# A three-layer transformer kernel on one core: gate rows read back from DRAM, and fewer closing steps on TensorE

## The chip, the cores and the metric

One of the cores of a Trainium2 chip runs the whole program. The metric is the device time of one execution in microseconds (us); lower is better. The core has TensorE (PE; its weight loads are shown apart as PEld), VectorE (DVE), ScalarE (ACT), GpSimd (POOL) and SyncE (SP), and 16 DMA engines that all queues share.

## The reference, cut to what matters

Two blocks run one after the other on a sequence of 256 tokens of width 1024. The first has two attentions and 16 experts. The second, in which the change lies, is this:

```python
for i in range(2):
    shift, scale, gate = adaln_params(c, ada_w[i, 0], ada_b[i, 0])
    hn = modulate(h, norm_g[i, 0], shift, scale)
    m = s5_mixer(hn, ...) if i == 0 else fox_mixer(hn, ...)
    h = h + gate * m
    shift, scale, gate = adaln_params(c, ada_w[i, 1], ada_b[i, 1])
    hn = modulate(h, norm_g[i, 1], shift, scale)
    h = h + gate * conv_ffn(hn, ...)
# end of s5_mixer:   y = gelu(y);  y = y * sigmoid(y @ w_glu);  return y @ w_out
# conv_ffn:          a, b = split(h @ w_up);  return (silu(conv3(a)) * b) @ w_down
```

The `gate` is one row of 1024 numbers for each of the four layers (S5, feed-forward 0, fox attention, feed-forward 1), the same for all tokens.

## The kernel before, in words

The stages run in this order: input projections and the two attentions of the first block; routing and 16 experts, whose weights stream from DRAM; S5; feed-forward 0; fox attention; feed-forward 1; the last norm. Each engine runs a list of instructions written out by hand, with waits on semaphores between the engines. TensorE's multiplications all go through the helper `mm` (line 705), its transposes of normed rows through `turn` (line 712).

**Weights.** They go through a ring of six slots of 2 MB. SP issues the loads in one fixed order (`weight_plan`), and each waits until the step that used its slot last is through (`released`). A weight is then split in two float32r parts, high on ACT (`apart_high`, line 508), low on DVE (`apart_low`, line 516), and TensorE makes three products (high by high, low by high, high by low) for each product of the reference. The two blocks of the S5 output weight are called ("s5", 4) and ("s5", 5). The second goes to the slots that ("s5", 2) had, the first block of `w_glu`, so it is loaded once `glu_mm` has reached 2.

**End of S5.** `y` comes in eight pieces, `ct` 0 to 7. Its first four and its last four are split separately: `y_high` on ACT (lines 1919, 1923), `y_low` on DVE (line 2807). The sums of `y @ w_glu` are made by `glu(i, half)`: `i` is the block of `w_glu`, `half` says which half of `y` goes in, and only the call with half 1 raises `glu_mm`, twice. ACT then makes the sigmoid of each bank (line 1931), DVE the product and its parts (lines 2844 to 2846), and TensorE multiplies by the output weight in four groups of 24 products, (t, n) = (0, 0), (0, 1), (1, 0), (1, 1). During S5 six blocks of `ada_w`, the weight behind shift, scale and gate, are loaded and multiplied (`ada_product`), one for each `ct`.

**Gate rows.** The results stand in `mod`, spread over partitions: element 128 c + p of a gate is on partition p. To multiply rows of tokens by it, it is needed as a row on every partition. `gate_rows` makes that on TensorE, with a product by the identity for each of 8 pieces, into two banks of PSUM, and ACT copies them to `GBs`, `GB` or `GBx` (lines 1927, 1968, 2031; `GB` and `GBx` are the tensor `adaS`). The DVE function `add_gated` (lines 2773 and 2774) multiplies a sum by the row and adds it to the residual `X`.

**Feed-forward.** 22 tiles of 128 columns, two to a step of the loop. For each tile TensorE has 48 products of `up` and 12 of `down`; ACT copies (line 1974) and makes the silu (1976), DVE the convolution, the product and its parts (2890 to 2898), and both split the next weights (1942, 1949; 2856, 2862). The four sums of `down` stay in banks 4 to 7 through all tiles. They are opened by a product of zeros in bf16 and closed by another one (`closed`), which raises `ffn_mm`; the closing products stand between the groups of three of the last tile.

Of the kernel before, what the change touches and what calls it, by code (L numbers as in the profile page):

```python
# [20 lines left out]
F32 = mybir.dt.float32  # L21
# [223 lines left out]
def build(nc, x, cons, cols, rows, relb, wrt, wff, bf16z, w_in, w_qb, w_kvb, w_o, w_gate, w_up, w_down, ada_w,  # L245
# [3 lines left out]
    sums_dram = nc.dram_tensor("forget_sums", [FH, T], F32).ap()  # L249

    with ExitStack() as ctx:
# [250 lines left out]
        def apart_high(act, n, halves=(0, 1)):  # L502

            name = APART[n]
            act.wait_ge(filled_sem[slot_of[name]], filled_at(*name))
            for half in halves:
                a = slice(half * SLOT // 2, (half + 1) * SLOT // 2)
                act.activation(ringr[:, high_slot[name], a], ring[:, slot_of[name], a], ACT.Copy  # L508
                               ).then_inc(S("w_high"), 1)
# [72 lines left out]
        def _(sp):  # L582
# [36 lines left out]
            for name, i in order:  # L619
                if name == "w_in":  # L620
                    a, n = Z_COLS[i]
                    s = begin(name, i)
                    if i == 0:
                        h = NC // 2 * n
                        sp.dma_start(ring[:, s, 0:h], w_in[:, 0:h]).then_inc(S("w_in_half"), 16)
# [49 lines left out]
                elif name == "s5":  # L675
                    load(begin(name, i), SLOT, block((s5_in, s5_glu, s5_out)[i // 2], i % 2))
# [20 lines left out]
        def _(pe):  # L697
# [93 lines left out]
            def gate_rows(layer, banks):  # L791

                for c in range(NC):
                    last = mm(ps[:, banks[c // 4], (c % 4) * P:(c % 4) * P + P],
                              mod[:, layer, 16 + c:17 + c].to_broadcast([P, P]), ident, True, True)
                last.then_inc(S("gate_mm"), 1)

# [17 lines left out]
            pe.wait_ge(S("w_in_half"), 16)  # L815
# [534 lines left out]
            glu(1, 0)  # L1350
            pe.wait_ge(S("mod_ready"), 1)
            pe.wait_ge(S("ada_kept"), 5)
            gate_rows(0, (6, 7))
            pe.wait_ge(S("y_low"), 2)
            glu(0, 1)
            glu(1, 1)


            pe.wait_ge(S("gate_copied"), 1)
# [20 lines left out]
            def ffn(k, turned):  # L1380
# [35 lines left out]
                def down(i, b, closing=False):  # L1416
                    pe.wait_ge(S("down_low"), i * 2 + (NF * k + b + 1))
                    pe.wait_ge(S("g_ready"), i * 2 + (NF * k + b + 1))
                    for i4 in range(4):
                        n, t = (i4 % 2, i4 // 2) if closing else (i4 // 2, i4 % 2)  # L1420
                        for g, w in ((gh, dh), (gl, dh), (gh, dl)):
                            last = mm(ps[:, 4 + 2 * n + t, :], g[:, b, t * P:t * P + P],
                                      w[:, b, BANK * n:BANK * n + BANK], False, False)
                        if closing and i4 < 3:
                            closed(4 + 2 * n + t)
                    last.then_inc(S("down_mm"), 1)
                    if closing:
                        closed(7)

                def closed(b):  # L1430

                    mm(ps[:, b, :], zb[0:1, 0:P], zb[0:1, :], False, True).then_inc(S("ffn_mm"), 1)
# [3 lines left out]
                gate_rows(2 * k + 1, (2, 3))  # L1436
# [64 lines left out]
            gate_rows(2, (2, 3))  # L1501
# [4 lines left out]
            pe.wait_ge(S("gate_copied"), 3)  # L1506
# [25 lines left out]
        def _(act):  # L1532
# [53 lines left out]
            def both_halves(k, r, layer, high):  # L1586
# [6 lines left out]
                for t in range(NT):  # L1593
                    features_high(k, t, high)

# [308 lines left out]
            for ct in range(NC):  # L1904
# [22 lines left out]
            act.activation(GBs.rearrange("p (b n) -> p b n", b=2), ps[:, 6:8, :], ACT.Copy  # L1927
                           ).then_inc(S("gate_copied"), 1)
# [6 lines left out]
            def ffn(k, turned, layer, roots, beside):  # L1935
# [9 lines left out]
                def down_high(i, b, first=False):  # L1945
                    ffn_filled(act, "down", k, b, i)
                    if not first:
                        act.wait_ge(S("down_mm"), i * 2 + (NF * k + b - 1))
# [18 lines left out]
                act.wait_ge(S("gate_mm"), layer + 1)  # L1967
                act.activation(GB.rearrange("p (b n) -> p b n", b=2), ps[:, 2:4, :], ACT.Copy
                               ).then_inc(S("gate_copied"), 1)
# [51 lines left out]
            def values_copied(j):  # L2021
# [8 lines left out]
            act.wait_ge(S("gate_mm"), 3)  # L2030
            act.activation(GBx.rearrange("p (b n) -> p b n", b=2), ps[:, 2:4, :], ACT.Copy
                           ).then_inc(S("gate_copied"), 1)
            values_copied(1)

# [188 lines left out]
        def _(v):  # L2223
# [626 lines left out]
            v.wait_ge(S("gate_copied"), 1)  # L2850

            def ffn(k, turned, layer, roots, added, beside):
# [61 lines left out]
                v.wait_ge(S("gate_copied"), layer + 1)  # L2914
# [61 lines left out]
            fox_low(7)  # L2976

# [105 lines left out]
```

## Time and profile before

| | us |
|---|---|
| median of three runs | 1316.57 (1311.68 to 1319.81) |
| the profiled execution | 1316.12 |
| its span | 1314.3 |
| mean granted clock of TensorE in it | 0.954 of full speed |

The profiled execution is longer than its span by 1.8 us, which lie around it. Busy time is what an engine did, not what bounds the kernel; the waits and the chain that ended last say that.

### The profile page before, as it was taken

To read this page: it belongs to the slowest core of one execution; us is meant where nothing else is said; L and a number is where in the kernel's file an instruction comes from. 1 tells how busy PE (TensorE), PEld (TensorE's weight loads), DVE (VectorE), ACT (ScalarE), POOL (GpSimd) and SP (SyncE) were. 2 spreads that over 40 slices of the span, in tenths; PEclk is the share of its full clock that TensorE was granted. 3 is DMA by queue.
4 is the path that set the end of the run, shared out by engine and by line. 5 is a ranking of instruction groups with operands and counts; after the bars stand their busy time and mean duration, and the time that the engine had idled before them with its cause. 6 is when DMAs were issued, how large, how long until landed. Compare 5 with 4: busy or idle time off the path is not lost.

```text
span 1314.3 us, 22196 instructions
## 1 busy us (share of the span) xinstructions
PE 1191.1 (91%) x8874; PEld 851.7 (65%) x8874; DVE 669.4 (51%) x1207; ACT 462.2 (35%) x746; POOL 168.1 (13%) x270
## 2 busy tenths in 40 slices
PE   8999899887789877787999999999999989999996
PEld 5646554432335323332877889999969767999995
DVE  3677452231211221121486757676675766667675
ACT  5463421010100001002654454444455545443343
POOL 0000115572343032101020000000000000000000
PEclk9999899898987899798999999999999999999998
DMA  9865599999999999999786465555456241554441
GB/s 372 356 222 244 230 404 418 430 428 428 428 428 428 428 429 428 429 428 428 291 349 231 161 272 203 181 191 191 176 193 240 82 160 49 187 192 184 178 178 40
DMA packets 38389, 371.81 MB, mean 283 GB/s; under 512 B 4133, under 2 KB 7742, under 8 KB 14398
## 3 DMA queue, kind: packets, MB, share of 16 engines
q1 hardware_dynamic: 34462, 365.47, 68.8%
q10 hardware_dynamic: 3872, 5.57, 1.2%
q8 instruction: 39, 0.64, 0.2%
q14 instruction: 16, 0.13, 0.0%
HBM read 369.94 MB, written 1.08 MB: 282 GB/s over the span
## 4 chain that ended last, share of the span: by engine, by line
PE 66%; DMA 23%; DVE 5%; ACT 3%; issue 2%; POOL 1%; DVEq 0%; SPq 0%; ACTq 0%
PE ps L705 64%; DMA ring<-in_w_up 20%; DMA ring<-in_ada_w 2%; PE ps L936 1%; DMA ring<-in_fox_out 1%; DMA ring<-in_s_out 1%; ACT XH L1617 1%; DVE X L2774 1%; DVE ring_parts L516 1%; ACT XH L1575 0%; PE ps L712 0%; DVE W L2955 0%; DMA X<-in_x 0%; PE ps L948 0%; DVE XH L2773 0%
## 5 line engine op out<-in xcount | busy, mean ns | idle before, releaser
L705 PE MATMUL ps<-W_parts 128*128 128x256 f32 (+2 forms) x2672 | 383.9, 305 | 3.9 <-DVE W_parts L2898 2.0
L705 PEld LDWEIGHTS ps<-W_parts 128*128 128x128 f32 x2672 | 356.8, 191 | 28.0 <-issue 4.1
L705 PE MATMUL ps<-ring,W 128*32 128x512 f32 (+2 forms) x1512 | 239.3, 679 | 55.2 <-DMA ring<-in_w_up 29.1
L705 PEld LDWEIGHTS ps<-ring,W 128*32 128x32 f32 (+1 forms) x1512 | 62.1, 124 | 190.8 <-issue 114.6
L705 PE MATMUL ps<-W 128*32 128x64 f32 (+7 forms) x1696 | 135.6, 290 | 23.9 <-DVE W L2755 12.8
L705 PEld LDWEIGHTS ps<-W 128*32 128x32 f32 (+5 forms) x1696 | 85.6, 152 | 78.3 <-issue 70.8
L2743 DVE COPY W<-ps 128x1024 f32<-128x1024 f32 x16 | 19.6, 1224 | 191.4 <-PE ps L705 191.4
L2856 DVE TENSOR_TENSOR W_parts<-ring,W_parts 128x2048 fp32r<-128x2048 f32 x44 | 100.8, 2292 | 26.2 <-ACT W_parts L1942 26.0
L705 PEld LDWEIGHTS ps<-kc,W 128*128 128x128 f32 x648 | 85.7, 212 | 28.2 <-DVE W L2743 17.4
L705 PE MATMUL ps<-kc,W 128*128 128x32 f32 (+2 forms) x648 | 88.1, 293 | 10.2 <-DVE W L2743 9.4
L705 PE MATMUL ps<-XH_parts,ring_parts 128*128 128x256 f32 x512 | 94.0, 286 | 2.1 <-ACT XH_parts L1578 1.9
L705 PEld LDWEIGHTS ps<-XH_parts,ring_parts 128*128 128x128 f32 x512 | 80.7, 193 | 6.0 <-ACT XH_parts L1578 3.9
L1942 ACT ACTIVATE W_parts<-ring 128x2048 fp32r<-128x2048 f32 x44 | 83.6, 1900 | 0.1
L516 DVE TENSOR_TENSOR ring_parts<-ring,ring_parts 128x2048 fp32r<-128x2048 f32 x27 | 60.8, 2283 | 25.4 <-ACT ring_parts L508 25.4
L705 PE MATMUL ps<-W_parts,ring_parts 128*128 128x256 f32 x256 | 73.1, 285 | 0.0
L705 PE MATMUL ps<-ring_parts,W_parts 128*128 128x512 f32 (+1 forms) x256 | 72.0, 397 | 1.0 <-DVE ring_parts L516 1.0
L508 ACT ACTIVATE ring_parts<-ring 128x2048 fp32r<-128x2048 f32 x28 | 52.4, 1907 | 30.3 <-DMA ring<-in_fox_in 12.5
L1828 ACT ACTIVATE W<-ps 128x1024 f32<-128x1024 f32 x16 | 16.4, 1023 | 126.6 <-PE ps L705 126.6
L2761 DVE TENSOR_TENSOR X<-X,ps 128x512 f32<-128x512 f32 x64 | 44.0, 687 | 28.9 <-PE ps L705 28.7
L1974 ACT ACTIVATE XH<-ps 128x256 f32<-128x256 f32 x44 | 16.8, 383 | 115.5 <-PE ps L705 115.5
L1847 ACT ACTIVATE W<-ps 128x512 f32<-128x512 f32 x16 | 9.6, 597 | 134.0 <-PE ps L705 134.0
L705 PEld LDWEIGHTS ps<-ring_parts,W_parts 128*128 128x128 f32 x256 | 47.8, 189 | 11.7 <-DVE ring_parts L516 1.4
(395 smaller groups left out, 1353.5 us busy)
## 6 DMA issues: line engine op xcount, KB each, us to landing
ring<-in_w_up SPq DMA_DIRECT2D x32, 2048.0 KB, 25.7
ring<-in_w_down SPq DMA_DIRECT2D x32, 2048.0 KB, 23.7
ring<-in_w_gate SPq DMA_DIRECT2D x29, 2048.0 KB, 24.0
ring<-in_ada_w SPq DMA_DIRECT2D x24, 2048.0 KB, 10.1
ring<-in_up SPq DMA_DIRECT2D x44, 1024.0 KB, 5.8
ring<-in_dn SPq DMA_DIRECT2D x44, 512.0 KB, 3.3
ring<-in_fox_in SPq DMA_DIRECT2D x6, 2048.0 KB, 7.9
ring<-in_w_o SPq DMA_DIRECT2D x2, 2048.0 KB, 15.7
```

Source lines behind the costliest of these rows:

```text
L508: act.activation(ringr[:, high_slot[name], a], ring[:, slot_of[name], a], ACT.Copy).then_inc(S("w_high"), 1)
L516: eng.tensor_tensor(ringr[:, slot_of[name], a], ring[:, slot_of[name], a], ringr[:, high_slot[name], a].bitcast(F32), ALU.subtract).then_i ...
L705: return pe.matmul(o, l, r, start=a, stop=z_, skip_group_check=True, **kw)
L936: last = pe.transpose(ps[:, 4 + g % 2, o:o + P], Pex[:, 2 * (g % 4) + h, kb * P:kb * P + P], ident)
L1617: act.activation(Pex[:, h, 0:n], src, ACT.Exp, bias=ngm[:, u, h:h + 1], scale=scale, accum_out=den[:, u, h:h + 1]).then_inc(S("exp_done"), 1)
L1828: act.activation(Gs.rearrange("p (b n) -> p b n", b=2), ps[:, 0:2, :], ACT.Copy).then_inc(S("g_copied"), 1)
L1942: act.activation(uh[:, b], ffn_raw("up", k, b).rearrange("p (a n) -> p a n", a=2), ACT.Copy).then_inc(S("up_high"), 1)
L1974: act.activation(apd[:, b, 2:2 + T], ps[:, b, 0:T], ACT.Copy).then_inc(S("a_copied"), 1)
L2743: v.tensor_copy(Us.rearrange("p (b n) -> p b n", b=2), ps[:, 2:4, :]).then_inc(S("u_copied"), 1)
L2761: tt(xs_part, xs_part, ps[:, k, :], ALU.add).then_inc(S("x_added"), 1)
L2774: tt(X[:, t, a], X[:, t, a], normed_rows[k][:, t, a], ALU.add).then_inc(S("x_gated"), 1)
L2856: tt(ul[:, b, :, :], ffn_raw("up", k, b).rearrange("p (a n) -> p a n", a=2), uh[:, b, :, :].bitcast(F32), ALU.subtract).then_inc(S("up_low ...
```

## The change

- `gate_rows`, its 8 products a layer and ACT's copies are gone. In their place ACT issues, for each layer, a DMA that writes the gate from `mod` to a new DRAM tensor (`gate_written`; the elements lie 4 bytes by 4 bytes: partition p holds elements p, 128 + p, ...) and later one that reads it back as a row onto 128 partitions (`gate_spread`). Layer 0 is written at `ct` 1 of S5 and read after the last `y_high`; layers 1 and 2 are written after the first two tiles of feed-forward 0, layer 3 after those of feed-forward 1; layers 1 and 3 are read before the last two tiles of their feed-forward, layer 2 after `values_copied(1)` of the fox stage.
- TensorE no longer waits for `gate_copied`; DVE does, at one more place (before the fox sums are added).
- The last of the three products of each closing group carries the closing mark and raises `ffn_mm`; `closed` is gone.
- ("s5", 5) is loaded in two halves with a semaphore each, and ACT splits its first half when that one is there.
- The gate sums of S5 go in the order glu(0, 0), glu(0, 1), glu(1, 0), glu(1, 1). Before: glu(0, 0), glu(1, 0), gate_rows, glu(0, 1), glu(1, 1).

```diff
@@ S5 on TensorE
-            glu(1, 0)
-            pe.wait_ge(S("mod_ready"), 1)
-            pe.wait_ge(S("ada_kept"), 5)
-            gate_rows(0, (6, 7))
             pe.wait_ge(S("y_low"), 2)
             glu(0, 1)
+            glu(1, 0)
             glu(1, 1)
-            pe.wait_ge(S("gate_copied"), 1)
+            pe.wait_ge(S("ada_kept"), 5)
@@ down, last tile
-                        for g, w in ((gh, dh), (gl, dh), (gh, dl)):
+                        for j, (g, w) in enumerate(((gh, dh), (gl, dh), (gh, dl))):
                             last = mm(ps[:, 4 + 2 * n + t, :], g[:, b, t * P:t * P + P],
-                                      w[:, b, BANK * n:BANK * n + BANK], False, False)
-                        if closing and i4 < 3:
-                            closed(4 + 2 * n + t)
-                    last.then_inc(S("down_mm"), 1)
-                    if closing:
-                        closed(7)
+                                      w[:, b, BANK * n:BANK * n + BANK], False, closing and j == 2)
+                        if closing:
+                            last.then_inc(S("ffn_mm"), 1)
+                    if not closing:
+                        last.then_inc(S("down_mm"), 1)
@@ feed-forward and fox on TensorE
                 up(0, 0, True)
-                gate_rows(2 * k + 1, (2, 3))
...
             values(0, 0, 0, 0, NC)
-            gate_rows(2, (2, 3))
             values(1, 0, 1, 0, NC)
...
-            pe.wait_ge(S("gate_copied"), 3)
@@ ACT
+            def gate_written(layer):
+                act.dma_start(bass.AP(gate_dram.tensor, layer * D, [[1, P], [P, NC]]), mod[:, layer, 16:24],
+                              allow_slow_non_contiguous=True).then_inc(S("gate_written"), 16)
+            def gate_spread(dst, layer, written):
+                act.wait_ge(S("gate_written"), 16 * written)
+                act.dma_start(dst, gate_dram[layer].partition_broadcast(P)).then_inc(S("gate_copied"), 16)
...
+                if ct == 1:
+                    gate_written(0)
...
+            gate_spread(GBs, 0, 1)
             apart_high(act, 4)
-            act.wait_ge(S("gate_mm"), 1)
-            act.activation(GBs.rearrange("p (b n) -> p b n", b=2), ps[:, 6:8, :], ACT.Copy
-                           ).then_inc(S("gate_copied"), 1)
...
                 tiles(0, True, True)
+                act.wait_ge(S("mod_ready"), 2 + k)
+                for row in (1, 2) if k == 0 else (3,):
+                    gate_written(row)
                 with act.Fori(1, NF // 2 - 1) as i:
                     tiles(i, True)
+                gate_spread(GB, layer, 3 + k)
                 tiles(NF // 2 - 1, False)
```

## Rows read from the trace of the kernel before

**Rows 1.** The page: the chain that ended last, by engine, share of the span.

```profile
PE 66%; DMA 23%; DVE 5%; ACT 3%; issue 2%; POOL 1%; DVEq 0%; SPq 0%; ACTq 0%
```

**Rows 2.** Windows, the feed-forwards: busy (x), granted clock, DMA share, GB/s.

```profile
772.00:960.00 188.00, 187.00 (x1327) 176.09 (x1327) 131.22 (x178) 82.17 (x93) 0.00 (x0) 1.00 0.52 195
1113.00:1301.00 188.00, 186.76 (x1326) 176.13 (x1327) 129.20 (x178) 80.01 (x91) 0.00 (x0) 1.00 0.44 162
```

**Rows 3.** Timeline of TensorE, gate rows: start, us, line, tiles; S5, feed-forward 0, fox.

```profile
726.80 1.95 PE L705 MATMUL ps<-kc,mod 128*128 128x128 f32 x16
...
777.81 1.95 PE L705 MATMUL ps<-kc,mod 128*128 128x128 f32 x16
...
1030.29 1.95 PE L705 MATMUL ps<-kc,mod 128*128 128x128 f32 x16
```

**Rows 4.** Timeline of DVE: the last `y_low`.

```profile
722.29 1.23 DVE L2807 TENSOR_TENSOR W_parts<-XH,XH_parts 128x1024 fp32r<-128x1024 f32 x1 [7.30 <-ACT XH_parts L1923]
```

**Rows 5.** Timeline of TensorE: start of glu(1, 0), then the S5 output groups.

```profile
720.96 0.36 PE L705 MATMUL ps<-XH_parts,ring_parts 128*128 128x256 f32 x1
...
739.89 5.75 PE L705 MATMUL ps<-ring_parts,W_parts 128*128 128x512 f32 x24
746.66 11.47 PE L705 MATMUL ps<-ring_parts,W_parts 128*128 128x512 f32 x48 [1.01 <-DVE ring_parts L516]
```

**Rows 6.** The chain that ended last, in order of time, around ("s5", 5).

```profile
734.47 7.86 DMA ring<-in_s_out
742.36 1.93 ACT ring_parts L508
```

**Rows 7.** Windows of 1 us around an idle time of TensorE; columns as in rows 2.

```profile
628.00:629.00 1.00, 0.00 (x0) 0.00 (x0) 0.92 (x3) 0.97 (x3) 0.00 (x0) 1.00 1.06 442
629.00:630.00 1.00, 0.20 (x2) 0.23 (x3) 1.00 (x2) 1.00 (x3) 0.00 (x0) 1.00 1.04 442
...
631.00:632.00 1.00, 1.00 (x7) 1.00 (x6) 0.08 (x1) 1.00 (x2) 0.00 (x0) 0.50 1.08 459
```

**Rows 8.** Timeline, the end of feed-forward 0: TensorE and DVE.

```profile
959.25 0.94 PE L705 MATMUL ps<-W_parts 128*128 128x512 f32 x3 [1.00 <-DVE W_parts L2898]
960.12 0.38 PE L705 MATMUL ps<-zb 1*128 1x512 bf16 x1
960.44 0.97 PE L705 MATMUL ps<-W_parts 128*128 128x512 f32 x3
960.61 0.69 DVE L2773 TENSOR_TENSOR W<-ps,adaS 128x512 f32<-128x512 f32 x1 [1.51 <-PE ps L705]
...
964.08 3.64 PE L705 MATMUL ps<-ring,silz 128*32 128x512 f32 x32
...
965.32 0.69 DVE L2774 TENSOR_TENSOR X<-X,W 128x512 f32<-128x512 f32 x1
```

**Rows 9.** Timeline of TensorE, the first fox scores.

```profile
1038.72 1.16 PE L705 MATMUL ps<-W 64*128 64x128 f32 x16 [0.90 <-DVE W L2955]
```

**Rows 10.** DMA queue q10 (ACT's): packets, MB, share; 998 to 1003 and 1003 to 1018.

```profile
q10 hardware_dynamic: 32, 0.02, 1.2%
...
q10 hardware_dynamic: 2064, 2.10, 42.4%
```

**Rows 11.** S5, an `ada_w` block: its issue, its time to landing, its product.

```profile
672.37 0.33 SPq L596 DMA_DIRECT2D ring<-in_ada_w  x1
...
ring<-in_ada_w SPq DMA_DIRECT2D x1, 2048.0 KB, 9.4
...
684.27 1.93 PE L705 MATMUL ps<-ring,silz 128*32 128x512 f32 x16
```

**Rows 12.** Feed-forward 0, an `up` tile: issue, time to landing, use on ACT.

```profile
789.74 0.34 SPq L616 DMA_DIRECT2D ring<-in_up  x1
...
ring<-in_up SPq DMA_DIRECT2D x1, 1024.0 KB, 7.5
...
797.93 1.90 ACT L1942 ACTIVATE W_parts<-ring 128x2048 fp32r<-128x2048 f32 x1
```

More of the change, by code:

```diff
@@ L249, in build @@
     sums_dram = nc.dram_tensor("forget_sums", [FH, T], F32).ap()
+    gate_dram = nc.dram_tensor("gate_rows", [LAYERS, D], F32).ap()
     with ExitStack() as ctx:
@@ L504, in apart_high @@
             name = APART[n]
-            act.wait_ge(filled_sem[slot_of[name]], filled_at(*name))
             for half in halves:
+                if name == ("s5", 5) and half == 0:
+                    act.wait_ge(S("half_filled"), 32)
+                else:
+                    act.wait_ge(filled_sem[slot_of[name]], filled_at(*name))
                 a = slice(half * SLOT // 2, (half + 1) * SLOT // 2)
@@ L624, in _ @@
                         h = NC // 2 * n
-                        sp.dma_start(ring[:, s, 0:h], w_in[:, 0:h]).then_inc(S("w_in_half"), 16)
+                        sp.dma_start(ring[:, s, 0:h], w_in[:, 0:h]).then_inc(S("half_filled"), 16)
                         sp.dma_start(ring[:, s, h:2 * h], w_in[:, h:2 * h]).then_inc(filled_sem[s], 16)
@@ L675, in _ @@
                 elif name == "s5":
-                    load(begin(name, i), SLOT, block((s5_in, s5_glu, s5_out)[i // 2], i % 2))
+                    src = block((s5_in, s5_glu, s5_out)[i // 2], i % 2)
+                    if i == 5:
+                        s = begin(name, i)
+                        sp.dma_start(ring[:, s, 0:SLOT // 2], src[:, 0:SLOT // 2]).then_inc(S("half_filled"), 16)
+                        sp.dma_start(ring[:, s, SLOT // 2:], src[:, SLOT // 2:]).then_inc(filled_sem[s], 16)
+                    else:
+                        load(begin(name, i), SLOT, src)
                 elif name == "up0":
@@ L789, in features @@
                             last.then_inc(S(sem), 1)
[L791 to L796, printed above, removed]
             pe.wait_ge(S("zeroed"), 1)
@@ L814, in _ @@
             wz = ring[:, slot_of["w_in", 0], :].rearrange("p (c n) -> p c n", c=NC)
-            pe.wait_ge(S("w_in_half"), 16)
+            pe.wait_ge(S("half_filled"), 16)
             pe.wait_ge(S("ht_act"), 1)
@@ L1947, in down_high @@
                     if not first:
-                        act.wait_ge(S("down_mm"), i * 2 + (NF * k + b - 1))
+                        act.wait_ge(S("down_mm"), i * 2 + ((NF - 1) * k + b - 1))
                     act.activation(dh[:, b, :], ffn_raw("down", k, b), ACT.Copy
@@ L1966, in ffn @@
                 down_high(0, 0, True)
-                act.wait_ge(S("gate_mm"), layer + 1)
-                act.activation(GB.rearrange("p (b n) -> p b n", b=2), ps[:, 2:4, :], ACT.Copy
-                               ).then_inc(S("gate_copied"), 1)
                 def tiles(i, ups, first=False):
@@ L2029, in _ @@
             apart_high(act, 12)
-            act.wait_ge(S("gate_mm"), 3)
-            act.activation(GBx.rearrange("p (b n) -> p b n", b=2), ps[:, 2:4, :], ACT.Copy
-                           ).then_inc(S("gate_copied"), 1)
             values_copied(1)
+            gate_spread(GBx, 2, 3)
             def fox_high(u):
@@ L2849, in _ @@
                 apart_low(v, 5, half)
-            v.wait_ge(S("gate_copied"), 1)
+            v.wait_ge(S("gate_copied"), 16)
             def ffn(k, turned, layer, roots, added, beside):
@@ L2913, in ffn @@
                 tiles(NF // 2 - 1, False)
-                v.wait_ge(S("gate_copied"), layer + 1)
+                v.wait_ge(S("gate_copied"), 16 * (layer + 1))
                 for j in range(4):
@@ L2976, in _ @@
             fox_low(7)
+            v.wait_ge(S("gate_copied"), 48)
             def fox_added(t, n):
```

2 lines of the change are left out of this document (removed).

## The prediction

> **What bounds the kernel now.** I read the page first: the chain of work that ended last goes through TensorE for 66% of the span, through DMA for 23%, through DVE for 5% [rows 1]. The DMA part is the experts' stage, which the change doesn't touch. Then the windows by stage: in both feed-forwards TensorE is busy 187 of 188 us at full clock, while the DMA engines are busy about half of the time [rows 2]. So there a product taken off TensorE is time taken off the kernel, and one more DMA is cheap. At the seams between the stages (end of S5, end of each feed-forward, start of the fox scores) it is the other way round: TensorE waits for DVE or ACT there, and a product taken off it only makes it wait longer. Each part of the change has to be read at its own place.
>
> **Gate rows off TensorE.** Each `gate_rows` is 8 products, seen as 16 passes, and takes 1.95 us [rows 3]. There are four.
> - Feed-forward 0 and 1: the products lie between the first and the second tile of `up`, in a stretch in which TensorE never rests [rows 2]. Gain 1.95 us each, 3.9 us together. What would be late next is the second tile's weights or the first tile's convolution; both have the 5.6 us of the next `up` tile before them and ACT loses its 1.03 us copy there, so I count nothing against the gain.
> - Fox: the products end at 1032.2, but the scores start at 1038.72 and wait 0.90 us for the last mask sum on DVE [rows 3, 9], whose chain has nothing to do with the gate rows. TensorE will wait 0.90 + 1.95 = 2.85 us instead. Gain 0.
> - S5: the products go, but so does the order around them (next part).
> - Added: four writes and four reads, issued by ACT. An issue of a DMA there costs its queue about 0.4 us; ACT has idle times of 2 us and more at each of these places, the copies of about 1.03 us that it loses are longer, and the reads land long before DVE needs them: 512 KB at S5 some 25 us ahead, in the feed-forwards two tiles, some 15 us. Cost 0, unless the writes hold up other loads (first rival). SP's list is not moved; nothing is queued on it behind the new DMAs except through the shared engines.
>
> **The order of the gate sums.** Before, glu(1, 0) starts at 720.96 [rows 5] and hides the wait for the second half of `y`: the last `y_low` runs on DVE from 722.29 for 1.23 us, so it is there at 723.5 [rows 4]. After, glu(0, 1) is next in line and TensorE must wait from 720.96 to about 723.6: 2.6 us. All the 144 products behind it are the same. Before, the sums and the gate rows end at 739.89 [rows 5]; that is 720.96 + 1.95 + 16.98 for three half sums. After: 723.6 + 17.0 = 740.6. So the new order loses 0.7 us at this point: the wait takes more than the place of the gate rows.
> In return `glu_mm` 2 comes at 723.6 + 5.6 = 729.2 and not at 734.4, and with it the load of ("s5", 5), which was issued at 734.47 and took 7.86 us [rows 6]. That load was late: ACT waited for it until 742.36, and TensorE stood 1.01 us at the second output group for the low part [rows 5, 6]. After, it has landed by about 737 in either form, so halving it adds nothing that the earlier start doesn't give. ACT splits it after the last sigmoid, from 741.3; the first half passes ACT (1.9 us) and DVE (2.3 us) by 745.5; the first output group ends at 740.6 + 5.75 = 746.3. The wait of 1.01 us goes. Net at the end of S5: +0.7 - 1.0 = -0.3 us.
>
> **The clock behind that wait.** The trace shows what a short rest of TensorE can do: after the windows 628 to 630, in which it was busy 0.20 of 2 us, it was at full clock first and then at 0.50 (1.2 in place of 2.4 GHz) in the window 631 to 632 [rows 7], in all for some 3.3 us. That costs about 1.65 us where TensorE sets the time. The page "TensorE: Matmul & The Clock Gate" of the Trainium skill (Part 1) says that the throttled clock is the default and that activity lifts it; the trace agrees in this row. The change adds three such rests: 2.6 us before glu(0, 1), 2.85 us before the fox scores, and one at the end of feed-forward 0 (below). The closest row is a rest of 1.8 us, and there the clock fell; so I take a fall in S5, +1.7 us. In the fox stage it already falls once after the scores begin; earlier or later makes no sure difference, 0 with 1.7 us either way.
>
> **The closing products.** A closing group is three products at 0.24 us each; with the product of zeros the groups start 1.19 us apart (959.25, 960.44) [rows 8]. Without it they start 0.72 us apart. But DVE takes 1.33 us for each of the four sums, so only the first one counts: DVE starts at 960.61, just after the zeros end at 960.50; in the change the third product ends at 960.19, so it starts at 960.30. Gain 0.31 us in each feed-forward, 0.6 us together. At the end of feed-forward 0 TensorE comes to the `ada_w` products (3.64 us, at 964.08 before [rows 8]) 1.9 us earlier and then has nothing to do for 2.1 us before the transposes: the third rest. I count no fall there; it is close.
>
> **Sum.** 3.9 (feed-forwards) + 0.3 (S5) + 0.6 (closings) = 4.8 us gained, 1.7 lost to the clock: 3.1 us net. Against the profiled execution: 1316.12 - 3.1 = 1313.0. This execution is 0.45 us under the median of the three runs (1316.57), which is nothing beside their spread of 8 us, so I leave the number at 1313.0.
>
> **Rival 1, slower: the writes of the gate rows choke the loads.** A gate is written in 1024 pieces of 4 bytes, 64 for each DMA engine. No row shows such a write. The nearest: ACT's queue moved 32 packets, half of them of 1 KB, in 1.2% of 16 x 5 us, 30 ns each, and 2064 packets of 1 KB in 42.4% of 16 x 15 us, 49 ns each [rows 10]. With p for one piece, a write takes 64 p of every engine. In S5 it falls into a row of loads with a slack of 684.27 - (672.37 + 9.4) = 2.5 us [rows 11]; in the feed-forward an `up` tile lands at 797.2 and is used at 797.93 [rows 12], and TensorE is a further 3.0 us behind ACT, together 3.7 us, for two writes in feed-forward 0 and one in feed-forward 1. Cost: (64 p - 2.5) + (128 p - 3.7) + (64 p - 3.7), each part at least 0. At 30 ns it is 0.1 us; at 49 ns 0.6 + 2.6 = 3.2 us; I take nothing, since a piece of 4 bytes carries less than the packets of both rows, and keep 3.2 us for the range. At p = 65 ns it would be 1.7 + 4.6 + 0.5 = 6.8 us, more than all the gain; this is where it decides. At 100 ns: 3.9 + 9.1 + 2.7 = 15.7 us, a time of 1328.7. At 120 ns 1334.
> The page "DMA: Bandwidth & Descriptors" of the Trainium skill speaks for this rival: by its rules for kernel authors a non-contiguous last dimension becomes one descriptor per element, and by its specifications a transfer under 512 B is done as a read, a change and a write. It gives no time for such an element; if that doubled the price of 49 ns, the time would be that of 100 ns above. No run of before shows such a write.
>
> **Rival 2: no fall of the clock.** The rest in S5 may lie so that the clock stays up: the trace has a rest of TensorE before the fox scores of 0.90 us without one, and the fall in rows 7 followed a rest that was cut in two. Then 1316.1 - 4.8 = 1311.3.
>
> **Rival 3: the gain is eaten.** The clock falls in S5 and again behind the 2.1 us rest after feed-forward 0 (3.3 us together), and a load is late by 1 to 2 us. Then 1316.1 - 4.8 + 3.3 + 1.5 = 1316.1, no change.
>
> **Rival 4: more than counted.** The clock stays up in S5 and the fall that the fox stage now has goes too, so that the second half of its chain, which hangs on a product made at half clock, moves up by 1.7 us, and the feed-forwards lose a wait or two of ACT: about 1309.
>
> **How the numbers follow.** Forecast with one fall 0.40; no fall 0.25; eaten 0.17; choked loads 0.09 (0.04 of it by less than 13 us above before); more than counted 0.09. The likeliest gives 1313. The range from 1308.5 to 1318 takes in all but the choked loads and the outer part of the runs' own spread. A measurement of this kernel can tell about 1% (13 us) from no change: faster by more than that would need 1303, which no case gives, 0.03; slower by more needs p of about 0.12 us, 0.05; within it 0.92.
>
> **What would show each step.** In the changed profile: no `ps<-kc,mod` rows; TensorE busy all through both feed-forwards, each 1.95 us shorter from its first `up` product to its last; a wait of TensorE for DVE line 2807 of about 2.6 us before glu(0, 1), and the window after it at 0.5 or at 1.0; the second output load issued near 729 and no wait for its low part; DVE's four sums starting 0.1 us after the third product; the fox scores starting after the same mask sum, with 2.9 us of rest before them; 1024 packets more for each gate, and their busy time, which gives p. The prediction is wrong if TensorE waits for an `ada_w` block in S5 or for a split weight in feed-forward 0, or if the reads of the gate rows come after DVE wants them.

## The result: slower by half a per cent, against a forecast of a small gain

The changed kernel takes 1323.98 us in the median of 17 runs (1316.32 to 1329.39), the kernel before 1316.9 us (17 runs, 1311.68 to 1323.1): a ratio of 1.0054, 95% interval 1.0036 to 1.0071. The forecast was 1313.0 us with a range up to 1318. So it is within 1% of the time before, but on the wrong side of it: 11.0 us above the forecast and 6.0 us above the end of the range.

The profiled execution of the changed kernel spans 1319.8 us against 1314.3 us. To see where the 5.5 us come from, I take the same TensorE products in both timelines as landmarks and write down the time from one to the next. The landmarks: the `ada_turn` products (`ps<-kc,adaS`) in S5, at 661.36, 702.01 and 720.04 us before, and the one after feed-forward 0, at 985.59; the first product of the S5 output [rows 5]; the first `up` product and the end of the last `down` product of each feed-forward; the first fox scores [rows 9].

| stretch, from landmark to landmark | before, us | after, us | difference |
|---|---|---|---|
| S5: `ada_turn` 1 to `ada_turn` 2 | 40.65 | 47.77 | +7.12 |
| `ada_turn` 2 to `ada_turn` 3 | 18.03 | 17.82 | -0.21 |
| `ada_turn` 3 to S5 output (the gate sums) | 19.85 | 22.15 | +2.30 |
| S5 output to first `up` | 32.10 | 30.82 | -1.28 |
| feed-forward 0, first `up` to last `down` | 191.84 | 189.03 | -2.81 |
| from there to its `ada_turn` | 21.76 | 23.05 | +1.29 |
| to the first fox scores | 53.13 | 53.03 | -0.10 |
| fox scores to first `up` | 74.52 | 72.83 | -1.69 |
| feed-forward 1 | 191.83 | 191.12 | -0.71 |
| from there to the end | 9.23 | 10.50 | +1.27 |

With 0.3 us that the execution is late at the first landmark already, these add up to 5.5 us. In the stretch from the fox scores to the first `up` TensorE waits for nothing that the change moved; it takes 72.8 to 76.2 us from one kernel's profile to another, with the granted clock in it at 0.98 to 0.91, so its 1.69 us are no gain of the change. The largest loss, more than the whole difference, is in one stretch that the forecast had at zero. Feed-forward 1 is the second place: it gained 0.71 us where feed-forward 0 gained 2.81.

**S5, the write of a gate row.** The page first, the chain that ended last, by engine:

```profile
PE 62%; DMA 24%; DVE 7%; ACT 3%; issue 2%; POOL 1%; SPq 0%; DVEq 0%; ACTq 0%
```

TensorE's share is lower than in [rows 1] (62% and 66%), DMA's and DVE's are a little higher. That fits work that waits for data; the rows below show where. The timeline of the changed kernel, rows that answer to [rows 11]: SP's issue of the `ada_w` block, ACT's issue of the write, TensorE, and the block's product:

```profile
672.70 0.33 SPq L600 DMA_DIRECT2D ring<-in_ada_w  x1
...
673.92 0.40 ACTq L1590 DMA_DIRECT2D gate_rows<-mod  x1
...
687.57 4.13 PE L715 MATMUL ps<-W 32*128 32x64 f32 x32 [0.24 <-issue]
691.62 3.19 PE L715 MATMUL ps<-ring,silz 128*32 128x512 f32 x16
```

The DMA view of the issues in 672 to 675: KB each, us from issue to landing:

```profile
ring<-in_ada_w SPq DMA_DIRECT2D x1, 2048.0 KB, 14.9
```

The block was issued 0.33 us later than in [rows 11] and its product ran 7.35 us later; it landed after 14.9 us and not after 9.4. The windows between (TensorE, its weight loads, DVE, ACT, POOL, clock, DMA share, GB/s):

```profile
674.00:682.00 8.00, 6.09 (x152) 4.32 (x149) 7.79 (x15) 2.94 (x5) 1.40 (x2) 1.00 0.87 332
682.00:684.00 2.00, 1.02 (x33) 0.85 (x25) 0.69 (x2) 0.00 (x0) 0.00 (x0) 1.00 3.20 131
684.00:686.00 2.00, 0.66 (x12) 0.56 (x13) 0.00 (x0) 1.37 (x3) 1.33 (x2) 1.00 0.00 0
686.00:688.00 2.00, 0.88 (x11) 0.73 (x14) 0.00 (x0) 1.65 (x3) 0.07 (x1) 0.85 0.53 41
688.00:692.00 4.00, 4.00 (x36) 3.41 (x36) 2.74 (x6) 0.00 (x0) 0.00 (x0) 0.50 0.59 221
```

and the queues in the first two of them:

```profile
q10 hardware_dynamic: 1014, 0.00, 7.1%
...
q1 hardware_dynamic: 16, 0.26, 319.0%
```

The prediction had no row for such a write; here it is. 1014 packets of 4 bytes took 7.1% of 16 x 8 us, 9 ns each, less than either price in [rows 10]. And still the loads stop. The 16 load packets that begin in 682 to 684, 16 KB each, took 319% of 16 x 2 us, 6.4 us each; in 684 to 686 no further packet begins (share 0.00, 0 GB/s). TensorE, ACT and POOL run dry, and after that idle time the clock is at 0.50. The price of the write is not its pieces' own time; it is the time by which the loads under way land later. I call this the hold.

The same hold meets the `up` tile in feed-forward 1, whose write was issued at 1134.01. ACT and TensorE:

```profile
1147.74 1.92 ACT L1943 ACTIVATE W_parts<-ring 128x2048 fp32r<-128x2048 f32 x1 [6.19 <-DMA ring<-in_up]
...
1152.04 8.31 PE L715 MATMUL ps<-W_parts 128*128 128x256 f32 x58 [2.36 <-DVE W_parts L2856]
```

The tile landed after 14.4 us. TensorE waits 2.36 us; in feed-forward 0 only 0.29 us, although there are two writes; there the two `up` tiles beside them landed after 12.3 and 12.8 us. An `up` tile took 7.5 us in [rows 12], so both feed-forwards have the hold, and most of it fits in the slack between a tile's landing and its use.

**The gate sums**, answering to [rows 4, 5, 7]: the last `y_low`, the wait before glu(0, 1), and the windows behind it.

```profile
729.52 1.23 DVE L2807 TENSOR_TENSOR W_parts<-XH,XH_parts 128x1024 fp32r<-128x1024 f32 x1 [7.08 <-ACT XH_parts L1927]
```

```profile
730.80 0.50 PE L715 MATMUL ps<-XH_parts,ring_parts 128*128 128x256 f32 x2 [2.47 <-DVE W_parts L2807]
```

```profile
732.00:734.00 2.00, 2.00 (x11) 2.00 (x11) 1.93 (x5) 1.98 (x2) 0.00 (x0) 0.50 0.00 0
734.00:736.00 2.00, 2.00 (x15) 2.00 (x14) 2.00 (x2) 0.90 (x2) 0.00 (x0) 0.70 0.03 8
```

The forecast wait was 2.6 us, the profile has 2.47, and the clock falls to 0.50 behind it, as forecast.

**The ends of the feed-forwards**, answering to [rows 8, 9]: the last group in one run of 12 products, DVE's first sum, the `ada_w` products; then the fox scores.

```profile
966.29 2.98 PE L715 MATMUL ps<-W_parts 128*128 128x512 f32 x12 [1.00 <-DVE W_parts L2898]
967.33 0.69 DVE L2773 TENSOR_TENSOR W<-ps,adaS 128x512 f32<-128x512 f32 x1 [1.19 <-PE ps L715]
...
969.20 3.64 PE L715 MATMUL ps<-ring,silz 128*32 128x512 f32 x32
...
974.98 1.97 PE L722 MATMUL ps<-kc,W 128*128 128x128 f32 x16 [2.13 <-ACT W L1559]
...
1045.35 1.70 PE L715 MATMUL ps<-W 64*128 64x128 f32 x16 [2.57 <-DVE W L2955]
```

DVE starts 1.04 us after the group where it was 1.36 us [rows 8]; the rest before the transposes is 2.13 us (forecast 2.1); the scores wait 2.57 us (forecast 2.85).

### The profile page after: what moved, and what is told of

It is laid out like the page before. It is cut to its first block, busy times and chain, and to the rows that moved or that the text cites. A ratio compares the mean times of both kernels' runs of the same rounds, so it can differ in the third digit from the quotient of the medians.

```text
span 1319.8 us, 22056 instructions
## 1 busy us (share of the span) xinstructions
PE 1186.0 (90%) x8802; PEld 846.4 (64%) x8802; DVE 670.1 (51%) x1207; ACT 458.6 (35%) x742; POOL 168.7 (13%) x270
## 4 chain that ended last, share of the span: by engine, by line
PE 62%; DMA 24%; DVE 7%; ACT 3%; issue 2%; POOL 1%; SPq 0%; DVEq 0%; ACTq 0%
PE ps L715 60%; DMA ring<-in_w_up 13%; DMA ring<-in_w_gate 6%; DMA ring<-in_up 2%; DMA ring<-in_s_in 2%; PE ps L939 1%; DMA ring<-in_fox_out 1%; ACT XH L1619 1%; DVE X L2774 1%; ACT XH L1567 0%; PE ps L722 0%; DVE W L2955 0%; DMA X<-in_x 0%; PE ps L951 0%; DVE W_parts L2856 0%
## 5 line engine op out<-in xcount | busy, mean ns | idle before, releaser
L715 PE MATMUL ps<-ring,W 128*32 128x512 f32 (+2 forms) x1512 | 242.4, 685 | 53.9 <-DMA ring<-in_w_up 29.3
L715 PE MATMUL ps<-W 128*32 128x64 f32 (+7 forms) x1696 | 138.4, 294 | 28.4 <-DVE W L2755 12.8
L1830 ACT ACTIVATE W<-ps 128x1024 f32<-128x1024 f32 x16 | 16.4, 1024 | 126.3 <-PE ps L715 126.3
```

The lines of the kernel that those rows point to most:

```text
L715: return pe.matmul(o, l, r, start=a, stop=z_, skip_group_check=True, **kw)
L1830: act.activation(Gs.rearrange("p (b n) -> p b n", b=2), ps[:, 0:2, :], ACT.Copy).then_inc(S("g_copied"), 1)
```

## The experiments

Theory A: the writes in 4-byte pieces hold the loads that share the engines with them. The rival to it is B: the loss belongs to the new order, the halves or late instructions. And for how the hold comes about there are three forms of A. A1: pieces that lie next to each other in DRAM; A2: their number; A3: any small write. Each run was timed beside the kernel before on the same chip (medians of before 1316.8 to 1317.3 us).

**1. Rows in 512-byte pieces.**

```diff
+                mm(ps[0:m, bank, 0:P], modf[:, 24 * l0 + 16:24 * l1], ident, True, True)
...
-                act.dma_start(bass.AP(gate_dram.tensor, layer * D, [[1, P], [P, NC]]), mod[:, layer, 16:24],
-                              allow_slow_non_contiguous=True).then_inc(S("gate_written"), 16)
+                own(act.activation(gT[0:m, :], ps[0:m, bank, 0:P], ACT.Copy))
+                act.dma_start(gate_dram[l].rearrange("(c n) -> c n", c=NC), gT[r:r + NC, :]
```

> The changed kernel, but the rows go out in other pieces: one product with the identity turns the 8 gate columns of a layer into 8 rows of 128 numbers (one for layer 0, one for layers 1 and 2, one for layer 3), ACT copies them out of PSUM, and each layer is written as 8 pieces of 512 bytes in place of 1024 pieces of 4 bytes. Everything else, the reads of the rows included, stays. Theory A (the 4-byte writes hold the loads behind them): the ada_w product that was 7.3 us late in S5 is on time again, the waits for the up tile in both feed-forwards go (1.05 us and 3.1 us lost there by the landmarks), together about 11.5 us: 1312.5 us against 1324.0 for the changed kernel, and 0.3% under the kernel before. The three products added cost 0.3 us. Theory B (the loss in S5 belongs to the new order, the halves or late instructions, and the writes only stand beside it): the stretch from 670 to 700 stays 7 us late and the time stays at 1320 or over.

Measured: 1316.9 us, ratio to before 0.9993 (0.9971 to 1.0015), so 7 us of the changed kernel's time are gone. By stages: `ada_turn` 1 to 2 takes 40.60 us (before 40.65), the `ada_w` block lands after 9.3 us, and neither feed-forward has a wait for a split weight (189.02 and 189.00 us). So the hold belongs to the writes, and B is out for this stretch. The product added is short; in feed-forward 0 it starts at 781.02 and the next tile's products at 781.36 (by the whole stage it costs 0.5 us: 189.0 us here and 188.5 in runs 5 and 7, which have neither this product nor a wait for a tile):

```profile
781.02 0.41 PE L717 MATMUL ps<-kc,mod 128*32 128x128 f32 x2
781.36 1.82 PE L717 MATMUL ps<-W_parts 128*128 128x256 f32 x13
```

But the time is 4 us above what I expected. In the profiled run the clock was at 0.62 in the window 704 to 708 and at 0.52 in 708 to 712, so that the stretch to `ada_turn` 3 took 20.46 us and not 18.0, and fell again after feed-forward 0 (24.19 us to its `ada_turn`, 23.05 in the changed kernel). Whether this kernel does so in every run, one profile can't tell.

**2. The closings alone**, on the kernel before.

```diff
-                        if closing and i4 < 3:
-                            closed(4 + 2 * n + t)
-                    last.then_inc(S("down_mm"), 1)
-                    if closing:
-                        closed(7)
+                        if closing:
+                            last.then_inc(S("ffn_mm"), 1)
+                    if not closing:
+                        last.then_inc(S("down_mm"), 1)
```

> The kernel before with one part of the change: the feed-forward sums are closed by their last product and not by a product of zeros. By the prediction 0.31 us in each feed-forward, 0.6 us together, 1316.3 us against 1316.9. By the rival that the rest of TensorE after feed-forward 0 (now 2.1 us) lets the clock fall: 1.7 us more in place of it, 1318.

Measured: 1314.25 us, ratio 0.9994 (0.9971 to 1.0018), no difference that can be told. By stages each feed-forward is 1.57 us shorter and what follows it longer. At the end of the kernel: 190.25 + 10.58 = 200.83 us where it was 191.83 + 9.23 = 201.06, a gain of 0.2 us (the spans are given to 0.1 us). After feed-forward 0: 190.28 + 24.16 = 214.44 us where it was 213.60; here the clock fell behind the rest:

```profile
967.26 3.47 PE L712 MATMUL ps<-kc,W 128*128 128x128 f32 x16 [2.12 <-ACT W L1562]
```

The same 16 transposes took 1.97 us in the changed kernel, after a rest of 2.13 us. The rest is the same, the fall is not: where it comes, the stretch to the `ada_turn` is 1.1 us longer (24.16 and 23.05).

**3. The new order alone**, on the kernel before, with the gate rows ahead of the wait.

```diff
-            glu(1, 0)
             pe.wait_ge(S("mod_ready"), 1)
             pe.wait_ge(S("ada_kept"), 5)
             gate_rows(0, (6, 7))
             pe.wait_ge(S("y_low"), 2)
             glu(0, 1)
+            glu(1, 0)
             glu(1, 1)
```

> The kernel before with one part of the change: the gate sums of S5 in the new order (glu(0, 1) before glu(1, 0)), while the gate rows stay on TensorE, ahead of the wait for y_low. By the prediction's working the rest before glu(0, 1) is 2.6 - 1.95 = 0.7 us, the clock stays up, the sums and rows end at 740.6 (0.7 us later), the wait of 1.0 us for the low part of the second output block goes: -0.3 us, 1316.6. By the rival that the order itself costs (the load of the block comes no earlier, or a clock fall in spite of the short rest): 1 to 2 us slower, 1318.5.

Measured: 1317.29 us, ratio 1.0005 (0.9984 to 1.0026). By stages: `ada_turn` 3 to the output 20.59 us (+0.74, forecast +0.7), from there to the first `up` 30.82 (-1.28, forecast -1.0), clock 1.00. The output block comes in one piece here, and 30.82 is the changed kernel's own figure: with the new order the halves add nothing, as forecast.

**4. The changed kernel with the old order.**

```diff
+            glu(1, 0)
             pe.wait_ge(S("y_low"), 2)
             glu(0, 1)
-            glu(1, 0)
             glu(1, 1)
```

> The changed kernel with the gate sums of S5 in the old order, so that glu(1, 0) covers the wait for y_low. If the rest of 2.5 us and the clock fall behind it cost what the prediction put on them (0.7 + 1.7 - 1.0 = 1.4 us), this is 1.4 us faster than the changed kernel: 1322.6, still 5.7 us over the kernel before, since the writes stay. If the order carries the loss instead, it is at 1317.

Measured: 1317.28 us, ratio 1.0007 (0.9989 to 1.0026). This is the rival's number, but the stages say why, and it is not the rival's reason alone. The hold is still there: the `ada_w` block lands after 14.2 us and `ada_turn` 1 to 2 takes 48.27 us. `ada_turn` 3 to the output takes 18.27 us against 22.15, a gain of 3.88 us; in feed-forward 1 the same write, issued 15.8 us after the first `up` product in both kernels, holds the `up` tile for less (it lands after 12.4 us, not 14.4) and costs TensorE 0.32 us and not 2.36; why the same write holds it by different times, these runs don't show. Together 5.9 us, where the medians are 6.7 us apart. The two profiled executions are only 4.5 us apart: other stretches of this one are longer, among them 0.93 us from `ada_turn` 2 to 3 and a wait of 0.82 us, in place of 0.29, in feed-forward 0. I had compared the order with the kernel before, in which the gate rows lie between the sums; with them gone the old order needs 18.27 us where it needed 19.85, and this gain is what the new order gives away, beside the wait and the clock.

**5 to 8. What it is in the write.** All are the changed kernel with the gate rows written in another shape; the reads in 5, 6 and 8 take another input, and in 7 the values come back in another order, so these four don't compute the reference.

```diff
-  bass.AP(gate_dram.tensor, layer * D,       [[1, P],   [P, NC]]),       mod[:, layer, 16:24]
+  bass.AP(gate_dram.tensor, layer * D * 128, [[128, P], [128 * P, NC]]), mod[:, layer, 16:24]   # 5
+  bass.AP(gate_dram.tensor, layer * D,       [[1, P],   [P, 1]]),        mod[:, layer, 16:17]   # 6
+  bass.AP(gate_dram.tensor, layer * D,       [[NC, P],  [1, NC]]),       mod[:, layer, 16:24]   # 7
+  bass.AP(gate_dram.tensor, layer * D * 16,  [[16, P],  [16 * P, NC]]),  mod[:, layer, 16:24]   # 8
```

5, elements 512 bytes apart:

> The changed kernel, but each 4-byte element of the gate rows is written 512 bytes behind the one before it (the tensor in DRAM is 128 times as large); the reads take a row of another input in place of the gate rows, so the output differs. Just as many pieces, just as small, at the same time. Theory A1 (the loads are held because all engines change neighbouring words of the same 4 KB of DRAM, each by a read, a change and a write): the stretch between the ada_turn products at 661 and 702 is back from 47.8 to about 40.6 us, and the wait for the up tile in feed-forward 1 goes. Theory A2 (the number of small writes sets it, wherever they go): the stretch stays at 47 to 48 us.

6, one eighth of the elements:

> The changed kernel, but of each gate only the first of 8 columns is written (128 pieces of 4 bytes in place of 1024); the reads take a row of another input, so the output differs. Theory A2 (a price for each piece): the hold of 7.1 us in S5 shrinks to about an eighth, and with the slack of 2.5 us before it nothing is left, 40.6 us between the ada_turn products. Theory A3 (any such write, long or short, makes the loads behind it wait once until it is closed): 45 us or more.

7, 32 bytes in each piece:

> The changed kernel, but each partition writes its 8 gate values next to each other: 128 pieces of 32 bytes in place of 1024 of 4, over the same 4 KB. The values of a row come back in another order, so the output differs. The run with an eighth of the elements held the loads as long as all of them did (13.9 us to land, 14.9 with all, 9.1 before), so the count is not the price. If it is that several engines change words of the same neighbourhood by read, change and write, 32-byte pieces side by side are held too: the ada_w load lands after 13 to 15 us and the stretch from 661 to 702 takes 46 us or more. If pieces of 32 bytes are past that, 9.3 us and 40.6 us.

8, elements 64 bytes apart:

> The changed kernel, but each 4-byte element is written 64 bytes behind the one before it (512 bytes apart the hold was gone: 9.2 us to land); the reads take another input, so the output differs. If a neighbourhood is as wide as a small write's own line of 64 bytes or less, the hold is gone here too: 9.2 us to land, about 41 to 43 us for the stretch from 661 to 702. If it is wider, up to 512 bytes, 8 elements still meet in each: 11 us or more to land, 44 us or more.

The landing of the `ada_w` block issued just ahead of the write, by the DMA view, in 5:

```profile
ring<-in_ada_w SPq DMA_DIRECT2D x1, 2048.0 KB, 9.2
```

in 6:

```profile
ring<-in_ada_w SPq DMA_DIRECT2D x1, 2048.0 KB, 13.9
```

in 7:

```profile
ring<-in_ada_w SPq DMA_DIRECT2D x1, 2048.0 KB, 9.6
```

in 8:

```profile
ring<-in_ada_w SPq DMA_DIRECT2D x1, 2048.0 KB, 9.4
```

| kernel | pieces | bytes each, distance | block lands, us | `ada_turn` 1 to 2, us | feed-forward 1, us | time, us (ratio to before) |
|---|---|---|---|---|---|---|
| changed | 1024 | 4, 4 apart | 14.9 | 47.77 | 191.12 | 1323.98 (1.0054) |
| 5 | 1024 | 4, 512 apart | 9.2 | 43.30 | 188.50 | 1313.76 (0.9976) |
| 6 | 128 | 4, 4 apart | 13.9 | 46.00 | 188.48 | 1319.71 (1.0024) |
| 7 | 128 | 32, 32 apart | 9.6 | 41.56 | 188.50 | 1314.07 (0.9974) |
| 8 | 1024 | 4, 64 apart | 9.4 | 40.61 | 188.50 | 1316.65 (0.9990) |

Run 6 decides against a price for each piece: 128 pieces hold the block nearly as long as 1024 do, 13.9 us and 14.9. The number is not wholly without effect: in feed-forward 1 the `up` tile beside its write lands after 9.3 us and TensorE doesn't wait, where it landed after 14.4 us in the changed kernel. Runs 5 and 8 decide for the place: the same 1024 pieces of 4 bytes, 512 or 64 bytes from each other, don't hold the block; of the 2.65 us that 5 is still above 40.65, the clock is a part (0.50 in its window from 692 to 694), and the rest is not explained. Run 7 was expected to be held and is not: pieces of 32 bytes side by side pass, and run 6 says that this is not for their number of 128. By their times against the changed kernel, 5, 7 and 8 are 7 to 10 us faster and 6 is 4 us faster. What is shown is that 4-byte pieces at neighbouring addresses stop the loads, and that 32-byte pieces and 64 bytes of distance don't. Nothing between 4 and 32 bytes, or between 4 and 64 bytes of distance, was run, and which step inside the memory or the engines it is, these runs don't show.

**9. The write alone**, on the kernel before; nothing reads it.

```diff
+                if ct == 1:
+                    act.dma_start(bass.AP(gate_dram.tensor, 0, [[1, P], [P, NC]]), mod[:, 0, 16:24],
+                                  allow_slow_non_contiguous=True).then_inc(S("gate_written"), 16)
```

> The kernel before with nothing but the write of layer 0's gate row added (1024 pieces of 4 bytes, issued by ACT behind the second tile of S5's loop; nobody reads it). By the theory that this write is what costs in S5: the stretch from 661 to 702 grows from 40.6 to about 47.8 us, and the whole kernel is 6 to 7 us slower, 1323.5. By the rival that the hold needs the changed kernel's other work: no change, 1317.

Measured: 1323.56 us, ratio 1.0047 (1.0031 to 1.0063). The block lands after

```profile
ring<-in_ada_w SPq DMA_DIRECT2D x1, 2048.0 KB, 14.2
```

and `ada_turn` 1 to 2 takes 46.03 us (47.8 were expected), the next stretch 18.87; all later stretches are those of before within 0.2 us. That is 6.2 us by the stages and 6.7 us by the medians. The profiled execution, 1324.88 us, is 8.8 us above that of before, but 2.7 us of this stand before the first landmark, where the write has not been issued. One DMA of 4 KB that nobody waits for costs about what the whole change costs; in the changed kernel its other gains and losses nearly cancel.

**10. The same 4-byte write at another time**, with the old order.

```diff
-                if ct == 1:
-                    gate_written(0)
+            gate_written(0)
             act.wait_ge(S("y_copied"), NC)
             act.activation(XNr[:, 4:8, :], HT[:, 4:8, :], ACT.Copy).then_inc(S("y_high"), 1)
-            gate_spread(GBs, 0, 1)
...
                                ACT.Sigmoid).then_inc(S("glu_sig"), 1)
+                if j == 0:
+                    gate_spread(GBs, 0, 1)
```

> The changed kernel with the gate sums of S5 in the old order, and with the write of the first gate row moved from behind the second tile of S5's loop to behind the last one, where the ada_w loads have landed, and its read behind the first sigmoid. The pieces stay 1024 of 4 bytes. If the write costs only because loads of ada_w stand behind it, the 7.1 us of S5 are back: against the kernel with the old order alone (1317.3) 7 us faster, 1310.3, unless the load of the first output block, issued there too, is held in their place (then 1314 to 1317).

Measured: 1310.56 us, ratio 0.9957 (0.9933 to 0.9981). The write and what moves beside it:

```profile
709.96 0.33 SPq L600 DMA_DIRECT2D ring<-in_s_out  x1
...
717.78 0.40 ACTq L1590 DMA_DIRECT2D gate_rows<-mod  x1
```

The last load has landed (after 8.6 us) when the pieces go out, and no other is in the queue until the second output block. `ada_turn` 1 to 2 takes 39.83 us. Nothing of the write's shape was changed; what counts in S5 is what shares the queues with it. The three writes of the feed-forwards stand where they stood, and the `up` tiles beside them are held here too: they land after 11.1, 13.2 and 11.9 us. In this execution that fits in the slack, and neither feed-forward loses more than 0.1 us (188.48 and 188.60 us).

**11. 512-byte pieces and the old order.** Runs 1 and 4 together.

> The changed kernel with rows written in 8 pieces of 512 bytes and with the gate sums of S5 in the old order: both causes taken away. By the stages of the profiles: S5's stretch to 702 as before, 1.6 + 1.3 us less from there to the first up tile, 2.8 us less in each feed-forward, 1.3 us more at each end of them: 5.9 us under the kernel before, 1311.0 us. If the clock falls in the stretch from 702 to 720 and after feed-forward 0 as in the run with 512-byte pieces (2.6 and 1.1 us), 1314.7.

Measured: 1311.15 us, ratio 0.9957 (0.9932 to 0.9982), as expected. `ada_turn` 3 to the output takes 18.28 us and the feed-forwards 188.98 and 189.00. Among the versions that compute the reference, runs 10 and 11 gain most on the kernel before (0.43%); run 12, below, has 0.26%.

**12. Run 10 with the second output block in one piece.**

```diff
-                if name == ("s5", 5) and half == 0:
-                    act.wait_ge(S("half_filled"), 32)
-                else:
-                    act.wait_ge(filled_sem[slot_of[name]], filled_at(*name))
+                act.wait_ge(filled_sem[slot_of[name]], filled_at(*name))
```

> The kernel with the old order of gate sums and the late write (1310.6), with the second output block of S5 loaded in one piece again. The stretch from the first output group to feed-forward 0 was 32.1 us before and 31.3 there. By the prediction's working (a load that starts earlier has landed in either form) it stays at 31.3 and the time at 1310.6. By the rival that in the old order the halves carry the gain: a wait for the low part comes back, 32.1 to 32.4 us, 1311.5.

Measured: 1314.34 us, ratio 0.9974 (0.9950 to 0.9997). The wait for the low part is back:

```profile
744.28 11.46 PE L707 MATMUL ps<-ring_parts,W_parts 128*128 128x512 f32 x48 [1.30 <-DVE ring_parts L517]
```

where run 10 has 0.24 us there; the stretch to the first `up` is 32.39 and not 31.34 us (30.82 in runs 4 and 11, which have the old order and the halves, and read the gate row earlier). So the rival was right: the halves give 1.05 us in the old order, and nothing in the new one, which starts the load early enough by itself. The medians are 3.8 us apart, more than this. A further part in the profile is feed-forward 1, 190.68 us: the write is the one of run 10, but here the `up` tile landed after 14.0 us, and TensorE waited for it:

```profile
1139.77 8.54 PE L707 MATMUL ps<-W_parts 128*128 128x256 f32 x59 [1.94 <-DVE W_parts L2848]
```

Landings after 11.9 (run 10), 12.4 (run 4), 14.0 and 14.4 us (changed kernel) go with waits of 0, 0.32, 1.94 and 2.36 us. So a 4-byte write left in a feed-forward costs between nothing and 2.4 us, and what sets it within these bounds stays open.

## Why the prediction was wrong, step by step

- **The step that failed** is in the first rival: "I take nothing, since a piece of 4 bytes carries less than the packets of both rows", and with it "Cost 0, unless the writes hold up other loads". The estimate of p was sound as far as it went, 9 ns measured. The form was wrong: a price for each piece, times 64, against a slack; with 9 ns the rival's own sum gives 0 us. One write of 4-byte neighbours made the load issued just ahead of it land 4.5 to 5.5 us later, with 128 pieces as with 1024, and cost 7.1 us in S5 in the changed kernel and 6.7 us by the medians of run 9. The mechanism, writes that hold up loads, stood among the rivals, but priced wrongly, with a chance of 0.09 and outside the range. The sign that the prediction named for being wrong came: the `ada_w` product in S5 ran 7.35 us late.
- **A rule beside it.** The page "DMA: Bandwidth & Descriptors" of the Trainium skill (rules for kernel authors) says that a non-contiguous last dimension becomes a descriptor for each element: the trace agrees, ACT's queue moved 1014 packets in 8 us where 1024 elements were written. Its specifications say too that a transfer under 512 B is a read, a change and a write; 4-byte pieces 64 or 512 bytes apart and 32-byte pieces are under that size as well and held nothing, so by these runs the size alone doesn't set the cost.
- **Gate rows off TensorE, 1.95 us each.** Right in kind, a little too large. From run 2 (190.28 and 190.25 us) to run 5, where no tile is late (188.48 and 188.50), it is 1.80 and 1.75 us. The 1.95 in [rows 3] is from the first start to the last end, and products overlap: in the trace of before, the product behind the group at 726.80 starts at 728.50, 1.70 us later. In feed-forward 1 the hold of the `up` tile then took 2.36 us back; the first rival had that place too.
- **Fox, 0.** Right: 53.03 us in place of 53.13, the wait is longer instead.
- **The order of the gate sums.** +0.7, -1.0 and +1.7 for the clock were forecast; run 3 gives +0.74 and -1.28, and the changed kernel 22.15 - 20.59 = 1.56 us more for the fall. Each term is within 0.3 us. That the fall came was the likelier case and not a sure one (0.40 against 0.25 without it), and run 1 had none. In weighing it the prediction took the rest of [rows 7] for one "cut in two" and of 1.8 us; the timeline of TensorE has it in one piece, 1.92 us long. What the step did not say is how much better the old order would have been once the gate rows are gone: 18.27 us, 3.9 less.
- **The halves.** "Adds nothing that the earlier start doesn't give" is right for the change as it stands (run 3) and wrong for the old order (run 12).
- **The closings.** Forecast -0.31 us each. Run 2 gives -0.2 us at the end of the kernel, and with the changed kernel's 23.05 us behind it feed-forward 0 would be 190.28 + 23.05 = 213.33, -0.27 us. Right. The third rest lets the clock fall in some profiles (runs 1, 2, 7 and 11 with 24.2 us to the `ada_turn`, not the changed kernel with 23.05), so "it is close" was a fair reading.
- **A slip in the chances.** "Slower by more needs p of about 0.12 us": by the rival's own sum about 0.10 us is enough (1328.7 us, 12.6 above before). No run had such a p, so nothing hangs on it.

With the hold put in, the sum is: -3.1 as forecast, +7.1 in S5, +2.4 and +0.3 in the feed-forwards, 6.7 us: 1316.12 + 6.7 = 1322.8, where the profiled execution took 1321.66 and the median is 1323.98. The three terms put in are the measured ones, so this shows that nothing large is left over; it is no second forecast.

## What to carry to other kernels

Price a new DMA by the loads beside it as well as by its bytes and pieces: 4 KB written as neighbouring 4-byte words held a 2 MB load for 5 us, and held none at a time when no load was queued. Turn such a row on TensorE first (one product, 0.5 us by the stage), or give each piece 32 bytes where the reader can take the values in that order, or move the write to where the queues are empty. And when a filler is taken out of an order, work out the old order without it before taking up a new one: here that was 3.9 us.

## What the runs showed of the hardware

- 4-byte writes to neighbouring addresses: 9 ns of an engine for each, and the 16 load packets of 16 KB that began in the window 682 to 684, when nearly all pieces had gone out, took 6.4 us each; 512 bytes apart, 64 bytes apart, or 32 bytes long, the load beside them was not held.
- The same rest of TensorE does not always end in a fall of the clock. After a wait of 2.47 us before glu(0, 1) it fell in the changed kernel and in runs 5 to 8 (`ada_turn` 3 to the output takes 22.13 to 22.39 us), and not in run 1 (20.60 us), whose TensorE shows the same wait and full clock in the windows behind it:

```profile
727.22 0.50 PE L717 MATMUL ps<-XH_parts,ring_parts 128*128 128x256 f32 x2 [2.47 <-DVE W_parts L2822]
...
728.00:730.00 2.00, 2.00 (x19) 2.00 (x18) 1.93 (x5) 1.98 (x2) 0.00 (x0) 1.00 0.03 8
```

- A rest of 2.12 to 2.13 us before the transposes was followed by 3.47 us for them in run 2 and 1.97 us in the changed kernel. What tells these apart stays open.
